# A two-layer decoder step on one core: six changes of order and form around its norms, its state table and its expert passes

## The reference

```
def rmsnorm(x, g):
    return x * rsqrt(mean(x * x, axis=-1) + EPS) * g

# layer 0: h = rmsnorm(x); S5 state space (32 groups, 64 complex states) beside sparse attention
#   the state recurrence h_t = Lbar h_{t-1} + Bbar u_t; then
#   x += mixer(h) @ w_out ;  x += swiglu(rmsnorm(x))            (d_ff 2816)
# layer 1: x += pool_mixer(rmsnorm(x))                          (trailing means over 2, 4, 8, 16)
def moe(h, router_w, w_gate, w_up, w_down):                     # h = rmsnorm(x), 8 experts, top 2
    logits = h @ router_w
    top_v, top_i = top_k(logits, 2)
    gates = softmax(top_v)
    for e in range(8):
        out += dense_gate[:, e:e+1] * swiglu(h, w_gate[e], w_up[e], w_down[e])   # d_ff 3584
```

## Time and profile before

| what | value |
|---|---|
| median of 3 runs | 1530.35 us (1525.0, 1530.35, 1530.5) |
| the profiled execution | 1525.81 us |
| its span in the trace | 1523.6 us, so 2.2 us lie around it |
| PE busy | 1469.6 us, 96% of the span |
| DVE, ACT, POOL busy | 1265.6, 985.4, 144.4 us |
| mean granted clock of PE | 0.974 of full speed |
| read from memory | 423.47 MB, 285 GB/s over the span |

### The profile page before, as it was taken

How to read it: one execution, slowest core, us unless ns; L and a number is a source line. 1 busy time by engine, 2 the same in 40 slices (tenths; PEclk the granted TensorE clock), 3 DMA queues, 4 the chain that set the end, 5 groups by cost and what they waited for, 6 DMA issues and landing times.

```text
span 1523.6 us, 22861 instructions
## 1 busy us (share of the span) xinstructions
PE 1469.6 (96%) x7443; PEld 1187.9 (78%) x7443; DVE 1265.6 (83%) x1669; ACT 985.4 (65%) x1295; POOL 144.4 (9%) x191
## 2 busy tenths in 40 slices
PE   6998899999998889999999999999999999999998
PEld 5664466999998568888888888888888888888886
DVE  8988994666644898889888889888888888988997
ACT  6111353544432677787787787778778778778774
POOL 2177700000000120000000000000000000001000
PEclk9998797999999999999999999999999999999999
DMA  6601253555464479999999999999999999999993
GB/s 238 237 28 56 62 179 134 174 166 169 141 179 160 158 285 387 371 365 371 379 352 380 366 371 375 370 364 371 372 371 357 379 376 359 372 380 362 383 394 125
DMA packets 217376, 434.84 MB, mean 285 GB/s; under 512 B 10673, under 2 KB 56909, under 8 KB 217052
## 3 DMA queue, kind: packets, MB, share of 16 engines
q1 hardware_dynamic: 212854, 416.99, 76.3%
q0 software_dynamic: 3840, 13.62, 2.4%
q10 hardware_dynamic: 622, 3.45, 0.6%
HBM read 423.47 MB, written 11.03 MB: 285 GB/s over the span
## 4 chain that ended last, share of the span: by engine, by line
PE 85%; DVE 4%; issue 1%; ACT 1%; DVEq 0%
PE bank L1451 21%; PE bank L1455 20%; PE bank L1456 20%; PE bank L1278 3%; PE bank L1282 3%; PE bank L1281 3%; PE bank L1476 2%; PE bank L1293 2%; PE bank L1297 1%; PE bank L1296 1%; PE bank L970 1%; PE bank L1229 1%; PE bank L1245 1%; PE bank L1113 1%; PE bank L1248 1%
## 5 line engine op out<-in xcount | busy, mean ns | idle before, releaser
L2356 DVE TENSOR_TENSOR split<-raw_w,split 128x1024 fp32r<-128x1024 f32 x672 | 783.6, 1219 | 50.1 <-ACT split L1822 48.9
L1822 ACT ACTIVATE split<-raw_w 128x1024 fp32r<-128x1024 f32 x672 | 688.9, 1061 | 105.1 <-PE bank L1451 103.9
L1451 PE MATMUL bank<-split,xgr 128*128 128x512 f32 x896 | 359.2, 401 | 6.1 <-DVE split L2356 6.0
L1455 PE MATMUL bank<-split,xgr 128*128 128x512 f32 x896 | 354.3, 395 | 0.0
L1456 PE MATMUL bank<-split,xgr 128*128 128x512 f32 x896 | 354.2, 395 | 0.0
L1451 PEld LDWEIGHTS bank<-split,xgr 128*128 128x128 f32 x896 | 169.0, 189 | 44.2 <-DVE split L2356 6.4
L1456 PEld LDWEIGHTS bank<-split,xgr 128*128 128x128 f32 x896 | 168.9, 188 | 40.2
L1455 PEld LDWEIGHTS bank<-split,xgr 128*128 128x128 f32 x896 | 169.1, 189 | 37.9
L1451 PE MATMUL bank<-split,hbr 128*128 128x512 f32 x448 | 178.7, 399 | 0.0
L1455 PE MATMUL bank<-split,hbr 128*128 128x512 f32 x448 | 176.9, 395 | 0.0
L1456 PE MATMUL bank<-split,hbr 128*128 128x512 f32 x448 | 176.8, 395 | 0.0
(11 more groups left out here) (450 smaller groups left out, 1844.2 us busy)
## 6 DMA issues: line engine op xcount, KB each, us to landing
raw_w<-in_moe_gate SPq DMA_DIRECT2D x112, 1024.0 KB, 7.2
raw_w<-in_moe_up SPq DMA_DIRECT2D x112, 1024.0 KB, 7.8
raw_w<-in_moe_down SPq DMA_DIRECT2D x112, 1024.0 KB, 7.1
ring<-in_w_gate SPq DMA_DIRECT2D x11, 1024.0 KB, 5.5
ring<-in_w_up SPq DMA_DIRECT2D x11, 1024.0 KB, 8.0
ring<-in_w_down SPq DMA_DIRECT2D x8, 1408.0 KB, 7.7
ring<-in_w_in SPq DMA_DIRECT2D x5, 2048.0 KB, 10.9
ring<-in_w_out SPq DMA_DIRECT2D x2, 2048.0 KB, 8.3
```

Source lines behind the costliest of these rows:

```text
L1451: first = mm(out, hi, place[:, s, 0, cols], start=start, stop=False)
L1455: mm(out, lo, place[:, s, 0, cols], start=False, stop=False)
L1822: A(place[:, s, 0, :], raw_w[:, at:at + BLOCK], ACT.Copy).then_inc(sem("high_ready"), 1)
L2356: TT(place[:, s, 1, :], raw_w[:, at:at + BLOCK], place[:, s, 0, :].bitcast(F32), ALU.subtract).then_inc(sem("low_ready"), 1)
```

## The change

Six edits:

1. **Slot numbers first.** POOL fills `slots_kept` right after an early memset instead of after the store of the rows.
2. **Rows stored by an adding transfer.** POOL no longer adds the two parts of `hn4`. It stores the high parts with three transfers, waits for them, and sends the rest with three more that add in memory.
3. **Third norm in columns.** PE forms the sums of squares with the squares as the stationary side and one column of ones as the moving side, three products for each chunk, so that the sums come out as columns of tokens. `stdT` goes away; ACT takes the roots of the columns, DVE their reciprocals. The order of `rank` and the last `h2n` changes too.
4. **Added squares.** For norms 1 and 2, POOL adds the squares of chunks 1 to 6 onto chunk 0 as they come, and PE sums two matrices instead of eight. Norm 1 is also moved behind the first gate and up.
5. **The table's last doubling shared.** For positions 128 to 255, ACT forms the cross terms for each group j with 32 activations of 128 x 128, and DVE finishes with 32 operations.
6. **Last pass by halves.** In the last pass the last `down` chunk is done for columns 0 to 511 and then for 512 to 1023; the first half's scatter runs before the last block of the second half. The output leaves in six stores.

The diff, cut to its core:

```diff
+HALF_TABLE = 128
-    f += [("wout", c) for c in range(1, C)] + ["norm1"]
+    f += [("wout", c) for c in range(1, C)]
     for i in range(FT):
-        f += [("gate", i), ("up", i)]
+        f += [("gate", i), ("up", i)] + (["norm1"] if i == 0 else [])
...
-    f += [("h2n", 0, 0), "stdT", "routerT", ("h2n", 0, 1)] + [("h2n", 1, 0), ("h2n", 1, 1), ("h2n", 2, 0), "rank", ("h2n", 2, 1)]
+    f += [("h2n", 0, 0), "routerT", ("h2n", 0, 1), ("h2n", 1, 0), ("h2n", 1, 1), "rank", ("h2n", 2, 0), ("h2n", 2, 1)]
...
 # SP, at the end
-            for t in range(TC):
-                sp.wait_ge(sem("rows_done"), 2 * t + 2)
-                sp.dma_start(o["y"][t * P:t * P + TCN[t], :], acc[0:TCN[t], t, :]).then_inc(sem("out"), 16)
+            for half in range(2):
+                cols = slice(half * 512, (half + 1) * 512)
+                for t in range(TC):
+                    sp.wait_ge(sem("rows_done"), TC * half + t + 1)
+                    sp.dma_start(o["y"][t * P:t * P + TCN[t], cols], acc[0:TCN[t], t, cols]).then_inc(sem("out"), 16)
...
 # POOL
+            def add_squares(k):
+                for c in range(1, C - 1):
+                    pool.wait_ge(sem("squares"), C * k + c + 1)
+                    TT(sqs[k][:, 0, :], sqs[k][:, 0, :], sqs[k][:, c, :], ALU.add).then_inc(sem("squares_added"), 1)
+                    pool.wait_ge(sem("squares_added"), (C - 2) * (k - 1) + c)
...
             nc.gpsimd.memset(hn4[:, :, 2, :].bitcast(F32), 0.0).then_inc(sem("hn_zeroed"), 1)
+            nc.gpsimd.tensor_copy(slots_kept, const("tok")[:, 2 * TC:2 * TC + 1]).then_inc(sem("slots_moved"), 1)
+            pool.wait_ge(sem("slots_moved"), 1)
...
-            link(nc.gpsimd.tensor_copy(rows4[0:24, 1, 2, :], parts[LOW_ROWS:LOW_ROWS + 24, 0, 2, :]))
             for t in range(TC):
-                remainder = parts[:, 1, t, :] if t < 2 else rows4[0:24, 1, 2, :]
-                last = TT(rows4[0:TCN[t], 0, t, :], parts[0:TCN[t], 0, t, :], remainder, ALU.add)
-            last.then_inc(sem("rows_summed"), 1)
-            pool.wait_ge(sem("rows_summed"), 1)
+                pool.dma_start(hn_rows[t * P:t * P + TCN[t], :], parts[0:TCN[t], 0, t, :]).then_inc(sem("hn_high_out"), 16)
+            pool.wait_ge(sem("hn_high_out"), 16 * TC)
             for t in range(TC):
-                pool.dma_start(hn_rows[t * P:t * P + TCN[t], :], rows4[0:TCN[t], 0, t, :]).then_inc(sem("hn_out"), 16)
-            pool.wait_ge(sem("pages_in"), 16)
+                remainder = parts[:, 1, t, :] if t < 2 else parts[LOW_ROWS:LOW_ROWS + 24, 0, 2, :]
+                pool.dma_start(hn_rows[t * P:t * P + TCN[t], :], remainder, accum_op=ALU.add).then_inc(sem("hn_out"), 16)
...
-            nc.gpsimd.tensor_copy(slots_kept, const("tok")[:, 2 * TC:2 * TC + 1]).then_inc(sem("slots_moved"), 1)
-            pool.wait_ge(sem("slots_moved"), 1)
...
 # PE
+            def added_norm_sums(k):
+                out = open_fill(f"norm{k}")
+                pe.wait_ge(sem("squares_added"), (C - 2) * k)
+                mm(out[:, 0:T], ones, sqs[k][:, 0, :], start=True, stop=False)
+                pe.wait_ge(sem("squares"), C * (k + 1))
+                mm(out[:, 0:T], ones, sqs[k][:, C - 1, :], start=False, stop=True).then_inc(full(f"norm{k}"), 1)
...
-            norm_sums(1)
             for f in range(FT):
+                if f == 1:
+                    added_norm_sums(1)
...
-            norm_sums(2)
+            added_norm_sums(2)
...
-                    last = mm(ps("norm3")[:, 0:T], ones, sqs[3][:, c, :], start=(c == 0), stop=(c == C - 1))
+                    for t in (0, 2, 1):
+                        last = mm(ps("norm3")[0:TCN[t], t:t + 1], sqs[3][:, c, t * P:t * P + TCN[t]], ones[:, 0:1],
+                                  start=(c == 0 and t == 0), stop=(c == C - 1 and t == 1))
...
+                    if kind == "down" and j == FC - 1 and not another:
+                        for q in range(4):
+                            down_block(j, q, (0,))
+                        for q in range(4):
+                            if q == 3:
+                                last_scatter(0)
+                            down_block(j, q, (1,))
+                        continue
...
 # ACT
+            act.wait_ge(sem("half_table"), 1)
+            for j in range(NJ):
+                A(crossed[:, 0, j, :], ei3[:, j, 0:HALF_TABLE], ACT.Identity, scale=turn_im[:, j:j + 1])
+                A(crossed[:, 1, j, :], er3[:, j, 0:HALF_TABLE], ACT.Identity, scale=turn_im[:, j:j + 1]).then_inc(sem("crossed"), 1)
...
-            root(3)
+            filled(act, "norm3")
+            A(std_col[:, 0:2], ps("norm3")[:, 0:2], ACT.Sqrt, bias=eps, scale=1.0 / D)
+            A(std_col[0:24, 2:3], ps("norm3")[0:24, 2:3], ACT.Sqrt, bias=eps[0:24, :],
+              scale=1.0 / D).then_inc(free("norm3"), 1)
...
 # DVE
+                if m == HALF_TABLE:
+                    link(nc.vector.tensor_copy(turn_at, er3[:, :, m - 1]))
+                    nc.vector.tensor_copy(turn_im, ei3[:, :, m - 1]).then_inc(sem("half_table"), 1)
+                    dve.wait_ge(sem("half_table"), 1)
+                    for j in range(NJ):
+                        dve.wait_ge(sem("crossed"), j + 1)
+                        STT(er3[:, j, m:2 * m], er3[:, j, 0:m], turn_at[:, j:j + 1], crossed[:, 0, j, :], ALU.mult, ALU.subtract)
+                        last = STT(ei3[:, j, m:2 * m], ei3[:, j, 0:m], turn_at[:, j:j + 1], crossed[:, 1, j, :], ALU.mult, ALU.add)
+                    link(last)
...
-            filled(dve, "stdT")
-            nc.vector.reciprocal(token_rs[:, 0:2], ps("stdT")[:, 0:2])
+            emptied(dve, "norm3")
+            nc.vector.reciprocal(token_rs[:, 0:2], std_col[:, 0:2])
...
+            nc.vector.tensor_copy(cur[:, TC:2 * TC].unsqueeze(1), pgate[:, bass.ds(n_pass, 1), :]).then_inc(sem("pass_cols"), 1)
+            dve.wait_ge(sem("pass_cols"), n_pass)
             for half in range(2):
...
-            nc.vector.tensor_copy(cur[:, TC:2 * TC].unsqueeze(1), pgate[:, bass.ds(n_pass, 1), :]).then_inc(sem("pass_cols"), 1)
-            dve.wait_ge(sem("pass_cols"), n_pass)
-            for k, b in enumerate(LAST_BANKS):
-                dve.wait_ge(bank_full[b], FIRST_FILL[b] + len(PASS_FILLS[b]) * n_last + (LAST_FILLS[b] + 1))
-                add_scattered(k, b).then_inc(sem("rows_done"), 1)
+                for t in range(TC):
+                    b = LAST_BANKS[TC * half + t]
+                    dve.wait_ge(bank_full[b], FIRST_FILL[b] + len(PASS_FILLS[b]) * n_last + (LAST_FILLS[b] + 1))
+                    add_scattered(2 * t + half, b).then_inc(sem("rows_done"), 1)
```

More of the change, by code:

```diff
@@ L1341, in _, with token_rows @@
             last_norm_sums(4, C)
-            def token_rows(kind, src, ts):
+            def token_rows(kind, src, ts, halves=(0, 1)):
                 for t in ts:
-                    for i in range(2):
+                    for i in halves:
                         out = open_fill((kind, t, i))
@@ L1353, in _ @@
             token_rows("h2n", h3, (0,))
-            out = open_fill("stdT")
-            emptied(pe, "norm3")
-            for t in range(TC):
-                last = mm(out[0:TCN[t], t:t + 1], std[0:1, t * P:t * P + TCN[t]], ones[0:1, 0:1], start=True, stop=True)
-            last.then_inc(full("stdT"), 1)
             emptied(pe, "router")
@@ L1364, in _ @@
             last.then_inc(full("routerT"), 1)
-            token_rows("h2n", h3, (1, 2))
+            token_rows("h2n", h3, (1,))
+            token_rows("h2n", h3, (2,), (0,))
             out = open_fill("rank")
@@ L1441, in pfull, with split_mm @@
                     return bank_full[PASS_BANK[name]]
-                def split_mm(outs, n, xs):
+                def split_mm(outs, n, xs, begins=True):
                     pe.wait_ge(sem("low_ready"), NBLK * i + n + 1)
                     s = n % PLACES
-                    begun = False
+                    begun = not begins
                     for hi, lo, out, cols, start, stop in xs:
@@ L1468, in down_block @@
                                slice(512 * half, 512 * half + 512), j == 0 and f == 0, j == FC - 1 and f == 3)
-                              for half in range(2)])
+                              for half in halves], begins=(0 in halves))
                 def hidden_T(j):
@@ L1518, in one_pass, with last_scatter @@
                             turn_rows(half)
+            def last_scatter(half):
+                past_emptied(pe, ("y", half), n_pass)
+                for t in range(TC):
+                    b = LAST_BANKS[TC * half + t]
+                    pe.wait_ge(bank_free[b], FIRST_FILL[b] + len(PASS_FILLS[b]) * n_last + LAST_FILLS[b])
+                    scatter_half(2 * t + half, b)
             with pe.Fori(0, n_last) as i:
@@ L1522, in _ @@
             one_pass(n_last, False)
-            for half in range(2):
-                past_emptied(pe, ("y", half), n_pass)
-            for k, b in enumerate(LAST_BANKS):
```

(18 more changed lines are left out.)

15 lines of the change are left out of this document (11 added, 4 removed).

## The result

The changed kernel takes 1513.74 us (median of 4 runs, 1512.61 to 1515.19), the kernel before 1529.62 us beside it (median of 4); the ratio is 0.9904, with a 95% interval of 0.9891 to 0.9918. A second set of runs on another occasion gave 1513.81 and 0.9907 (0.9893 to 0.9921). The forecast was 1513.5 us, with a range of 1507.5 to 1520.5. It is faster by 0.96%, beyond the 0.5% that such runs can tell. So the total is right, but it is a sum of six terms, and two of them, the stall's and the clock's, are not what I took them for. One execution of e5 and one of e9 ran in a slow state (2443 and 3665 us); they are left out, and the medians given for these two are of the other three.

What follows compares the result with a forecast made beforehand. PE bounds the dense layer and passes, with one large stall between; 2.0 + 2.3 + 1.5 + 6.1 + 1.8 + 0.8 = 14.5 us gives 1511.3 (profiled) or 1515.9 (median), so 1513.5 us, range 1507.5 to 1520.5.

Steps and rivals of the forecast that it cites:

- the stall's: PE's 5.96 us wait before pass 0's sixth block: 6.1 us gained, 5.15 from POOL's hold on DVE, 0.9 from norm 3.
- the clock's: Behind the sixth block of pass 0: with a wait of only 0.8 us the clock stays up, 1.8 us come back.
- Edit 3: Norm 3 in columns: without the way back over PE, DVE's chain to pick shifts 0.9 us earlier, bounds -0.1 and 1.3.
- I take 0: Norm 3's column products and loads on PE: no net cost for the four chunks on the path, bounds -0.4 and +1.0.
- The adding transfer: Row stores on POOL: three more issues and a later end are covered by about 60 us before the gather, cost 0.
- Rival C: Adding transfer is slow: POOL stands until it lands, PE waits at the turn of the rows, kernel could be slower; chance 0.02.
- Edit 4: Added squares: fewer PE passes gain 2.3 us at norm 1 and 1.5 us at norm 2.
- Edit 5: Table's last doubling: ACT's 32 activations at 0.30 us each let DVE's first state tile start 2.0 us earlier.
- Edit 6: Last pass: scatter products ahead of the last block gain 0.7 us, smaller stores 0.1, together 0.8 us.
- A: The stall stays: PE still waits 4 us or more before the sixth block, gain 7.5 us; chance 0.09.
- B: Weight stream in pass 0 has no room and eats some 3 us, gain 11.5 us; chance 0.09.
- D: Shared table doubling or added squares cost: table -0.6 us, norm 1 only 1.0, total gain 10.6 us; chance 0.10.

Runs made afterwards that it cites:

- e5: Changed kernel with the table's last doubling made by DVE alone again, as before; 1515.69 us, ratio 0.9923.
- e9: Changed kernel with the last pass in whole blocks again, scatter and additions behind the last down, rows stored whole; 1515.31 us, ratio 0.9913.
- e2: Changed kernel with POOL copying and adding the row parts again instead of the adding transfer, slot numbers still early; 1521.36 us, ratio 0.9961.
- e6: Changed kernel with the count of passes loaded into DVE's and ACT's registers behind the pass loop instead of ahead of it; 1513.28 us, ratio 0.9905.
- e10: Changed kernel without the second register load on PE, DVE, ACT and POOL, the count of passes worked out from the last pass's number; 1513.07 us, ratio 0.9898.
- e1: Changed kernel with the third norm in rows again, with stdT and the old order of token rows and rank; 1515.23 us, ratio 0.9922.
- e8: Changed kernel with norms 1 and 2 by sixteen products again, norm 1 ahead of the first gate, no adds on POOL; 1519.60 us, ratio 0.9940.
- e4: Changed kernel with an added all-ones product per chunk beside the third norm's column products, its result never read; 1517.29 us, ratio 0.9936.

## Why the prediction was right, and where it was not

- **Edits 1 and 2, stall (6.1 us forecast, of it 5.15 for DVE's hold).** Counted from the last `pool` product, block 5 comes 2.49 us earlier (33.79 for 36.28), not 6.1. The hold itself is right in mechanism (e2) and in size: from `pick` to the end of its tables DVE takes 11.45 us for 16.62, 5.17 less. The first failed sentence is "and I leave them as they are": I took DVE's register loads as 2.17 us, the gap of before, and they grew to 3.45, the first from 0.78 to 1.39 us, which takes 1.28 back. The other 1.40 us are lost before `pick`, by edit 3 and the clock (the next two points): 5.17 - 1.28 - 1.40 = 2.49. PE's own second load grew as well and put block 0 0.29 us later behind `pick` (7.14 for 6.85), so that 1.81 us of its wait stayed for 0.8, and blocks 0 to 5 take 4.2 us less. Taking one load away took 1.3 us back (e6). The diff's first edit brings 0.6 us only with the second one, and nothing alone, as "ACT's wait alone would not have mattered" had it.
- **Edit 3 (0.9 us inside the stall's term).** This step failed. At full clock `pick` comes at +16.29 from the last `pool` product in e10 and at +16.21 in the rows form (before and e1). The chunk of columns takes 1.34 us on PE against 1.24, four chunks 0.4 us, and PE waits 0.28 us for ACT's copy of the router: together that pays back the trip of `stdT`. DVE's reciprocals do come 0.73 us earlier in e10 than before, but DVE then waits 0.85 us for the router's rows. My "I take 0" was the mis-sized term, and it lay within its bound of +1.0; the shift of 0.9, too, went to its lower bound of -0.1. The load of the third with 24 columns is short, as the prediction has it (that pair of products takes 0.14 us, a pair with 128 columns 0.31), but the four chunks lost 0.4 us and did not gain the 0.3 worked out with it.
- **The clock (1.8 us).** Failed as a net gain. Undoing the removal of the stall does bring a fall of 2.7 us (e2), and behind block 5 the changed kernel gains 1.65 us on the kernel before, for 1.8. But with the stall gone, a fall came at 508 us, and `pick` is 1.3 us later than in e10, which had none (block 0 is 1.85 us later, of which 0.5 is PE's second register load). So 0.3 us are left of 1.8. Between 480 and 560 us the mean granted clock is 0.91 before and 0.91 after. My list of signs asked only about the stretch behind block 5.
- **The adding transfer (cost 0).** Right. POOL's scatter stands at 541.31 and the first gather at 593.56, earlier than before. Rival C has nothing for it. e2 without it is slower.
- **Edit 4 (2.3 and 1.5 us).** Right in both parts, 2.6 and 1.3 in e8. The low parts were not lengthened (0.50 and 1.23 us, as in e8). But that says nothing of what an add beside them costs, for they hardly met: POOL's adds, 0.80 us each, fell into DVE's idle time (around norm 1 its waits of 1.45 us for ACT), and only two of the twelve overlapped a product of DVE, by 0.17 and 0.06 us. PE came to the last two chunks of gate 0 too early and lost some 0.5 us there in four steps, where the forecast gave back 0.35.
- **Edit 5 (2.0 us).** Right where it was worked out: ACT's 32 activations start 0.29 us apart, for the 0.30 taken, and the gain is 1.84 us at PE's first state product (1.97 in e5), with ACT's first 8 columns as the new limit and DVE waiting 1.66 us for them. What of it reaches the end stays open.
- **Edit 6 (0.8 us).** Right, 0.9 in e9.
- **The bounds.** The lower bounds of the terms add up to a gain of 2.4 us and the upper ones to 16.3; "about 11 to 17" is thus a judgement and not their sum.
- **The rivals.** A did not come, though a small part of it did, on DVE in place of ACT: register loads kept 1.81 us of wait. B did not come: ahead of all the gate and up products of the passes PE stood 2.2 us in all, 1.81 at block 5 for DVE and 0.42 at block 0 behind its own loads. Nor did D.

The span's 12.2 us follow from the shift between the two profiled traces, step by step: 1.84 us at the first state tile, 1.51 more by the output projection (the clock's chance), 2.33 at norm 1, 1.55 at norm 2, 2.32 from there to block 5, 1.65 behind block 5, 1.0 at the end. So the stall, edit 3 and the clock gave 4.0 us where I had 7.9, and chance gave 1.5 where I had nothing. The medians are 15.9 us apart, since the profiled execution of before lay 3.8 us below its median and that of after 0.5 us. That my figure, put between the two sums, came within 0.3 us of the median is luck: the sum was 2.3 us too large for the pair of traces and 1.4 too small for the pair of medians, and the figure had been put between the two.

## What to carry to other kernels

Before a stall's lost clock is counted as won, look for the next light stretch: in a chain of small products and waits the fall tends to come there. Filling the light place (e4) or taking the light products out (e1) only moved it to the next wait; of the column form's nine traces one, e10, had none. A releaser in a profile is only the last semaphore seen; where the named engine had finished long ago, read the chain piece by piece, since register loads of the waiting engine's own hide in such a gap. Compare a stage from its own first product, and profile the unchanged code twice, before a difference of 2 us between two traces is given to an edit.

## What the runs showed of the hardware

- A register load from SBUF on DVE took 0.33 to 1.42 us at the same place in the code: 0.78 and 0.33 before, 0.77 and 0.33 in e2, 1.39 and 0.99 in the changed kernel, 1.42 for the only one in e6 and e10, each with 0.2 us of sequencer time behind it. The long ones fall in stretches with a DMA share near 1 (1.00 and 1.18 in the changed kernel), the short ones of before at 0.60 and 0.00. PE's second load goes the same way, 0.32 us at a share of 0.00 before and 0.73 at 1.02 in the changed kernel; POOL's do not, 0.50 and 0.30 us in both. That is what stands beside them; that the transfers cause it was not tried. The Trainium skill (Runtime: NRT & Kernel Launch, "Instruction fetch mechanics") gives some 0.2 us a register for TENSOR_LOAD; these, which the trace shows under that name, all took longer.
- Products with one moving column cost 0.13 us each on average at full clock (six in 0.77 us: 0.31 for each pair with 128 stationary columns, 0.14 for the pair with 24), and the same instructions let the clock fall in 8 of 9 traces and not in the ninth.
- The four row stores of 512 KB, two plain and two adding, landed a median 4.5 us after issue, the two of 96 KB, one plain and one adding, 6.4 us. The plain ones of before took 3.4 and 3.9 us. What an adding one takes by itself the view does not tell.
